# A depthwise convolution shared by four engines: fp32 taps lead on TensorE, VectorE goes on in its bank, and one more low part comes by transfer

## The chip, the cores and the metric

The kernel runs on one core of a Trainium2 chip. The metric is device time in microseconds, from one launch; lower is better. Engines: TensorE (PE, with its weight loads as PEld), VectorE (DVE), ScalarE (ACT), GpSimd (POOL) and SyncE (SP), which issues loads. SBUF and PSUM have 128 partitions; PSUM has 8 banks of 512 fp32 columns.

## The reference

A decoder trunk over 512 positions of 1024 channels, in fp32, two layers, each a token mixer and a gated ConvFFN. Only the first mixer matters here:

```python
def conformer_conv_module(x, w_in, b_in, w_dw, b_dw, ln_g, ln_b, w_out, b_out):
    h = x @ w_in + b_in
    a, gate = jnp.split(h, 2, axis=-1)
    h = a * jax.nn.sigmoid(gate)
    h = causal_depthwise_conv(h, w_dw, b_dw)     # 31 taps over positions, each channel by itself
    h = jax.nn.silu(layer_norm(h, ln_g, ln_b))
    return h @ w_out + b_out
```

After it come the residual norm, the first ConvFFN, the gMLP mixer and the second ConvFFN.

## The kernel before, in words

**Products in split precision.** A matmul of fp32 accuracy is written as three products of `float32r` parts: each operand has a high part (`wh`, `xh`: a copy rounded to float32r) and a low part (`wl`, `xl`: the rest). The weights come in 160-odd units of 128 x 1024. A unit is loaded by SP into one of four slots of `raw` (L464), its high part is made by ScalarE (`his`, L668 to L676), its low part either by a VectorE subtraction (`los`, L1045) or, for the units in `BY_DMA` (L94; 5 to 17), so: ScalarE also writes the negated rounded copy into `wl` (L676), and an accumulating transfer issued by GpSimd (`lo`, L538 to L541) adds `raw` to it. SP loads unit u into its slot only once the low part of unit u - 4 is there (`lo_of`).

**The convolution stage** has eight tiles of 128 channels. Units 2j (gate) and 2j + 1 (value) make tile j: 24 products of 512 columns each, into banks 0 to 2 in turn (`unit_conv`, L1652). ScalarE takes the sigmoid (L773), VectorE multiplies (`gated_channels`, L1080) into `glu[j % 2]`, 30 zeros ahead of 512 positions. The 31 taps of the tile are then shared:

- TensorE has the last `PE_TAPS[j]` taps (5, and 8 in tile 6) as products with diagonal matrices, three products a tap from the split parts `gluh`, `glul`, `diagh`, `diagl` (`taps`, L1683 to L1702), into bank 4 + j % 2.
- VectorE has 17 taps, alternately in banks 6 and 3 (L1108, L1111, L1114), each reading and writing its bank.
- ScalarE makes 9 products (6 in tile 6) into SBUF (`products`, L733), and GpSimd adds them into `gsum` (L550).
- VectorE closes the tile: `gsum` plus its two banks (L1125), plus TensorE's bank, into `cbuf` (L1132; counted by `conv_c`). It also makes `glul` (L1086) from ScalarE's `gluh` (L786).
- TensorE transposes `cbuf` (`to_tm`, L1709) and ScalarE copies that out to `ctm` (L758).

The diagonal matrices of tiles 0 and 1 come from GpSimd (L568), the others from ScalarE, two halves a tap (L713, L714). Tile 7 has its own code, in two halves of 256 positions (`last_taps`, `last_products`, `add_last`, `own_taps`): 17 and 20 taps on TensorE, whose diagonals GpSimd makes for 15 taps (`POOL_LAST`) and ScalarE for the rest. Behind it stand the norm's statistics, the transposes back to feature order (`to_fm`, L1765), silu and its parts (L834, L837, L1205), and the output product (L1618 to L1620).

**What sets the order** is each engine's program as written out by hand, with semaphores between them. TensorE runs unit 2, unit 3, unit 4, `taps(0)`, unit 5 and so on (the loop at the end of the listing). SP's queue in the first 22 us holds the first units, x, parameters, and then the residual's four `res` tiles (L487) and three broadcast rows (L488 to L490).

## Time and profile before

| | us |
|---|---|
| median of 3 runs (lowest, highest) | 1035.72 (1035.41, 1037.11) |
| the profiled execution | 1036.58 |
| its span, first to last instruction | 1034.6 |
| TensorE busy in the span | 1022.5 (99%) |
| VectorE busy | 812.4 (79%) |
| ScalarE busy | 513.0 (50%) |
| GpSimd busy | 233.9 (23%) |
| granted TensorE clock, mean | 0.999 of full speed |
| HBM read, written | 178.11 MB, 54.53 MB |

The span is what the profile covers; the 2 us beside it lie around the first and last instruction. Matmuls are pipelined: a record runs from its start to a modelled end, so that starts, not durations, give their cost. A line number is that of the listing. Times within the span count from its start.

### The profile page before, as it was taken

What the parts mean: (1) busy time and instruction counts of PE and PEld (TensorE: products, weight loads), DVE (VectorE), ACT (ScalarE), POOL (GpSimd) and SP (SyncE); (2) the same over time, 40 slices, a digit from 0 to 9 for tenths busy, and PEclk for the clock granted to TensorE, in tenths of its full rate; (3) what the DMA queues carried; (4) which work ended last, traced back from release to release, by engine and by line L of the source; (5) the groups of instructions that cost most, each with busy time, mean ns of one, the idle gap of its engine ahead of it and who ended that gap; (6) DMA issues with size and microseconds to landing.
All of it is one profiled execution on the core that took longest, in us unless ns stands there. A gap on an engine that the chain in (4) does not pass through costs nothing.

```text
span 1034.6 us, 14305 instructions
## 1 busy us (share of the span) xinstructions
PE 1022.5 (99%) x4799; PEld 854.8 (83%) x4799; DVE 812.4 (79%) x1163; ACT 513.0 (50%) x773; POOL 233.9 (23%) x286
## 2 busy tenths in 40 slices
PE   8999999999999999999999999999999999999997
PEld 7788888988888888888888888898888888888885
DVE  6999977687777776788895778758777677778888
ACT  6899965334343333466553443333433343346553
POOL 2988750413341000000010110042334000000001
PEclk9999999999999999999999999999999999999999
DMA  9566349999998233286555433879999623327653
GB/s 336 169 161 154 91 120 311 227 245 278 229 254 203 84 101 101 82 284 203 186 183 183 140 102 107 305 159 269 282 232 248 168 81 101 101 82 264 203 190 115
DMA packets 65003, 189.70 MB, mean 183 GB/s; under 512 B 7488, under 2 KB 8512, under 8 KB 64960
## 3 DMA queue, kind: packets, MB, share of 16 engines
q1 hardware_dynamic: 44144, 137.76, 39.0%
q0 software_dynamic: 18800, 44.05, 21.8%
q10 hardware_dynamic: 2016, 7.34, 2.1%
q8 instruction: 24, 0.39, 0.2%
q14 instruction: 19, 0.16, 0.0%
HBM read 178.11 MB, written 54.53 MB: 225 GB/s over the span
## 4 chain that ended last, share of the span: by engine, by line
PE 92%; DVE 4%; DMA 1%; issue 1%; ACT 1%; SPq 1%; POOL 0%; DVEq 0%; POOLq 0%; ACTq 0%
PE ps L1608 19%; PE ps L1610 19%; PE ps L1609 19%; PE ps L1851 6%; PE ps L1849 6%; PE ps L1850 6%; PE ps L1618 4%; PE ps L1620 4%; PE ps L1619 4%; DMA raw<-d_weights 1%; PE ps L1779 1%; DVE ps L1114 1%; PE ps L1700 1%; PE ps L1701 1%; PE ps L1699 1%
## 5 line engine op out<-in xcount | busy, mean ns | idle before, releaser
L1608 PE MATMUL ps<-xh,wh 128*128 128x512 f32 x816 | 317.7, 389 | 0.3 <-DVE wl L1045 0.3
L1609 PE MATMUL ps<-xl,wh 128*128 128x512 f32 x816 | 317.5, 389 | 0.0
L1610 PE MATMUL ps<-xh,wl 128*128 128x512 f32 x816 | 317.5, 389 | 0.0
L1608 PEld LDWEIGHTS ps<-xh,wh 128*128 128x128 f32 x816 | 153.2, 188 | 32.3 <-DVE wl L1045 0.8
L1610 PEld LDWEIGHTS ps<-xh,wl 128*128 128x128 f32 x816 | 153.2, 188 | 32.0
L1609 PEld LDWEIGHTS ps<-xl,wh 128*128 128x128 f32 x816 | 153.2, 188 | 31.8
L674 ACT ACTIVATE wh<-raw 128x1024 fp32r<-128x1024 f32 x114 | 119.9, 1056 | 81.7 <-PE ps L1851 63.4
L1045 DVE TENSOR_TENSOR wl<-raw,wh 128x1024 fp32r<-128x1024 f32 x101 | 122.9, 1222 | 41.9 <-ACT wh L674 41.9
L528 POOL TENSOR_SCALAR veps<-sqs 128x1 f32<-128x1 f32 x15 | 5.7, 380 | 554.1 <-ACT squares L849 554.1
L1341 DVE TENSOR_TENSOR wl<-raw,wh 128x1024 fp32r<-128x1024 f32 x80 | 97.6, 1220 | 7.7 <-ACT wh L903 7.6
L1851 PE MATMUL ps<-wh,parts 128*128 128x512 f32 x264 | 102.7, 389 | 0.0
L1849 PE MATMUL ps<-wh,parts 128*128 128x512 f32 x264 | 102.7, 389 | 0.0
L1850 PE MATMUL ps<-wl,parts 128*128 128x512 f32 x264 | 102.7, 389 | 0.0
L886 ACT ACTIVATE vpad<-ps,par 128x512 f32<-128x512 f32 x44 | 30.3, 690 | 143.2 <-PE ps L1610 140.9
L615 POOL DMA_DIRECT2D summed<-d_weights x88 | 73.5, 1100 | 107.8 <-DMA summed<-d_weights 94.5
L894 ACT ACTIVATE parts<-made (+1 forms) x44 | 18.4, 418 | 134.7 <-DVE made L1320 134.7
L903 ACT ACTIVATE wh<-raw 128x1024 fp32r<-128x1024 f32 x80 | 84.1, 1051 | 2.1 <-DMA raw<-d_weights 2.1
L1313 DVE SCALAR_TENSOR_TENSOR gacc<-gpad,par,gacc 128x512 f32<-128x512 f32 x88 | 66.1, 752 | 12.7 <-DVE gacc L1309 6.2
L1313 DVE SCALAR_TENSOR_TENSOR vacc<-vpad,par,vacc 128x512 f32<-128x512 f32 x88 | 66.1, 752 | 11.9
L550 POOL TENSOR_TENSOR gsum<-gsum,prods 128x512 f32<-128x512 f32 x53 | 69.4, 1309 | 10.4 <-ACT prods L733 4.0
L1114 DVE SCALAR_TENSOR_TENSOR ps<-glu,par,ps 128x512 f32<-128x512 f32 x105 | 70.0, 747 | 0.0
L1309 DVE TENSOR_SCALAR vacc<-vpad,par 128x512 f32<-128x512 f32 x44 | 24.0, 546 | 46.6 <-ACT vpad L886 46.6
(201 smaller groups left out, 1738.3 us busy)
## 6 DMA issues: line engine op xcount, KB each, us to landing
raw<-d_weights SPq DMA_DIRECT2D x156, 512.0 KB, 4.1
raw<-summed SPq DMA_DIRECT2D x56, 512.0 KB, 3.4
summed<-d_weights POOLq DMA_DIRECT2D x88, 256.0 KB, 8.6
summed<-d_weights SPq DMA_DIRECT2D x66, 256.0 KB, 7.9
summed<-summed POOLq DMA_DIRECT2D x46, 256.0 KB, 5.1
wl<-raw POOLq DMA_DIRECT2D x13, 512.0 KB, 5.0
...
```

Of the source, the lines that this page charges most:

```text
L674: eng.activation(split_at(u)[0], raw[:, u % RAW, :], ACT.Copy).then_inc(w_hi, 1)
L903: eng.activation(wh[:, slot, :], raw[:, part, :], ACT.Copy).then_inc(w_hi, 1)
L1045: eng.tensor_tensor(l, raw[:, u % RAW, :], h.bitcast(f32), ALU.subtract).then_inc(w_lo, 1)
L1114: eng.scalar_tensor_tensor(out=own[k % 2], in0=glu[:, j % 2, k:k + SEQ], scalar=par[:, c:c + 1], in1=own[k % 2], op0=ALU.mult, op1=ALU.add ...
L1313: eng.scalar_tensor_tensor(out=sums_v[:, :], in0=buf[:, off:off + SEQ], scalar=par[:, bass.ds(cw, 1)], in1=sums_v[:, :], op0=ALU.mult, op1 ...
L1341: eng.tensor_tensor(wl[:, slot, :], raw[:, part, :], wh[:, slot, :].bitcast(f32), ALU.subtract).then_inc(w_lo, 1)
L1608: eng.matmul(ps[:, bank, cols], a, xh[:, k, cols], start=(k == 0), stop=False)
L1609: eng.matmul(ps[:, bank, cols], a, xl[:, k, cols], start=False, stop=False)
L1610: mm = eng.matmul(ps[:, bank, cols], b, xh[:, k, cols], start=False, stop=(k == KD - 1))
L1849: eng.matmul(ps[:, bank + t, :], s_h, w_h[:, cols], start=first, stop=False)
L1850: eng.matmul(ps[:, bank + t, :], s_h, w_l[:, cols], start=False, stop=False)
L1851: mm = eng.matmul(ps[:, bank + t, :], s_l, w_h[:, cols], start=False, stop=last)
```

## The change

Tile 0 has no taps on TensorE, tiles 1 to 5 have three and tile 6 eight, each as one fp32 product (`diagf` with `glu`) ahead of the units, not behind them. VectorE goes on with its taps in TensorE's bank (`CHAIN`) and in one bank of its own (`SUMS[j % 2]`), which ScalarE begins with one tap (`begun`); in tile 0 ScalarE begins both banks. VectorE gates tile j + 1 before the last two taps of tile j, and closes a tile in two steps (`close_sum`, `close_chain`), the second after the first tap of the next tile. `gluh`, `glul`, `diagh` and `diagl` remain for tile 7 alone. The low part of unit 4 too comes by transfer, and units 6 to 15 have one transfer for two units. TensorE now runs units 2, 3, 4 and then, for j from 1 to 5, taps of tile j, unit 2j + 3, `to_tm(j - 1)`, unit 2j + 4; then unit 15, taps of tile 6, `to_tm(5)`. The diff, cut to its core:

```diff
-PE_TAPS = [5, 5, 5, 5, 5, 5, 8] + [20]
+CHAINED = KD - 2
+PE_TAPS = [0] + [3] * (CHAINED - 1) + [8] + [20]
 GP_TAPS = [9, 9, 9, 9, 9, 9, 6]
...
-LAST_AT = 11
-UNIT_4_AT = 10
-
-POOL_TILES = 2
+LAST_AT = 10
...
-BY_DMA = range(LEAD + 2, U_CONV_OUT + 2)
+BY_DMA = range(LEAD + 1, U_CONV_OUT + 2)
+
+LO_DMAS = [[LEAD + 1], [LEAD + 2]] + [[u, u + 1] for u in range(LEAD + 3, U_CONV_OUT, 2)] + [[U_CONV_OUT], [U_CONV_OUT + 1]]
+LO_DMA = {u: d for d in LO_DMAS for u in d}
...
     SUMS = (6, 3)
+    CHAIN = (4, 5)
     CT = 7
...
-            eng.wait_ge(w_neg, u - BY_DMA[0] + 1)
-            eng.dma_start(split_at(u)[1], raw[:, u % RAW, :], accum_op=ALU.add).then_inc(lo_in[u % RAW], 16)
+            n, slot, q = len(LO_DMA[u]), u % RAW, u % RING
+            eng.wait_ge(w_neg, u + n - BY_DMA[0])
+            eng.dma_start(wl[:, q:q + n, :], raw[:, slot:slot + n, :], accum_op=ALU.add).then_inc(lo_in[slot], 16)
 
...
+        n = PE_TAPS[1]
+        w = par[:, C_CDW_W + TAPS + PE_FROM[1]:C_CDW_W + 2 * TAPS].rearrange("p (n o) -> p n o", o=1).broadcast_to([P, n, P])
+        eng.wait_ge(par_in, 16)
+        eng.affine_select(out=diagf[1][:, 0:n, :], in_=w, compare_op=ALU.is_equal, fill=0.0,
+                          base=0, pattern=[[0, n], [-1, P]], channel_multiplier=1).then_inc(diag_p, 1)
+        add_products(0, range(1, 4))
+        lo(LEAD + 1)
+        add_products(0, range(4, 6))
+        lo(LEAD + 2)
+        add_products(0, range(6, GP_TAPS[0]))
         eng.wait_ge(dw_ok, 2)
-        diagonals(0, 0, PE_TAPS[0])
-        add_products(0, range(1, AT_ONCE))
-        diagonals(1, 0, PE_TAPS[1])
-        add_products(0, range(AT_ONCE, GP_TAPS[0]))
-        last_at = PE_TAPS[KD - 3]
+        last_at = 0
         for j in range(1, KD):
-            for u in (2 * j + LEAD, 2 * j + 1 + LEAD):
-                if u in BY_DMA and u < BY_DMA[-1]:
-                    lo(u)
             if j < KD - 1:
+                lo(2 * j + LEAD + 1)
                 add_products(j, range(1, GP_TAPS[j]))
...
+                if j < KD - 1:
+                    if j > 2 and q < PE_TAPS[j - 2]:
+                        eng.wait_ge(dw_pe, j - 2)
+                    last = eng.activation(diagf[j % 2][:, q, :], ident[:, :], ACT.Copy, scale=w)
...
+        def begun(j, k, bank):
+
+            if j == CHAINED:
+                eng.wait_ge(conv_c, j - 1 + k)
+            elif j >= 2:
+                eng.wait_ge(conv_c, j - 1)
+            c = C_CDW_W + j * TAPS + k
+            eng.activation(ps[:, bank, :], glu[:, j % 2, k:k + SEQ], ACT.Copy, scale=par[:, c:c + 1]).then_inc(own_ok, 1)
...
+        sigmoid(0)
+        eng.wait_ge(glu_s, 1)
+        begun(0, 1, SUMS[0])
+        products(0, 0, 2)
+        begun(0, 0, CHAIN[0])
+        products(0, 2, 4)
+        his([LEAD + 1])
+        products(0, 4, 5)
+        his([LEAD + 2])
+        products(0, 5, 7)
+        sigmoid(1)
+        his([LEAD + 3])
+        products(0, 7, GP_TAPS[0])
+        his([LEAD + 4])
+        for j in range(1, CHAINED):
             eng.wait_ge(glu_s, j + 1)
+            begun(j, 0, SUMS[j % 2])
+            products(j, 0, 4)
             if j >= 2:
...
-                his([1 + LEAD])
+            products(j, 4, 6)
...
+            if j + 1 < CHAINED:
+                diagonals(j + 1, range(PE_TAPS[j + 1]))
+            else:
+                diagonals(j + 1, range(PE_TAPS[j + 1] // 2))
+            products(j, 6, GP_TAPS[j] - 1)
+            sigmoid(j + 1)
+            his([2 * j + LEAD + 3])
+            products(j, GP_TAPS[j] - 1, GP_TAPS[j])
+            if j + 1 < CHAINED:
+                his([2 * j + LEAD + 4])
+            else:
+                diagonals(j + 1, range(PE_TAPS[j + 1] // 2, PE_TAPS[j + 1]))
+        j = CHAINED
+        eng.wait_ge(glu_s, j + 1)
+        begun(j, 0, SUMS[0])
+        products(j, 0, 2)
+        begun(j, 1, SUMS[1])
+        products(j, 2, 3)
+        ct_out(j - 2)
+        products(j, 3, AT_ONCE)
+        diagonals(j + 1, range(sum(POOL_LAST), sum(POOL_LAST) + 2))
+        sigmoid(KD - 1)
+        products(j, AT_ONCE, GP_TAPS[j])
+        diagonals(j + 1, range(sum(POOL_LAST) + 2, PE_TAPS[KD - 1]))
         eng.wait_ge(glu_s, KD)
...
+        def chain_of(j):
+
+            if j == 0:
+                return [(k, SUMS[0] if k % 2 else CHAIN[0]) for k in [3] + [k + d for k in range(2, DV_TAPS[0] - 2, 2) for d in (3, 0)] + [DV_TAPS[0] - 2]]
+            if j == CHAINED:
+                return [(k, SUMS[k % 2]) for k in [2, 4, 3] + list(range(5, DV_TAPS[j]))]
+            return [(k, SUMS[j % 2] if k % 2 else CHAIN[j % 2]) for k in range(1, DV_TAPS[j])]
+
...
+        def close_sum(j):
+
+            bank = SUMS[j % 2]
+            eng.wait_ge(dw_tap, ended[j, bank])
             eng.wait_ge(gp_add, adds_before(j + 1))
-            for part in own:
-                n = stat(eng.tensor_tensor(gsum[:, j % 2, :], part, gsum[:, j % 2, :], ALU.add))
-                if part is own[0] and 0 < j < KD - 2:
-                    gated_low(j + 1)
-                eng.wait_ge(st_ok, n)
-            eng.wait_ge(dw_pe, j + 1)
+            return stat(eng.tensor_tensor(gsum[:, j % 2, :], ps[:, bank, :], gsum[:, j % 2, :], ALU.add))
+
+        def close_chain(j, n):
+
+            bank = CHAIN[j % 2]
+            c = C_CDW_B + j
+            eng.wait_ge(dw_tap, ended[j, bank])
+            eng.wait_ge(st_ok, n)
             if j >= 2:
                 eng.wait_ge(ct_pe, j - 1)
-            eng.tensor_tensor(cbuf[:, j % 2, :], gsum[:, j % 2, :], pe_bank, ALU.add).then_inc(conv_c, 1)
+            eng.scalar_tensor_tensor(out=cbuf[:, j % 2, :], in0=gsum[:, j % 2, :], scalar=par[:, c:c + 1],
+                                     in1=ps[:, bank, :], op0=ALU.add, op1=ALU.add).then_inc(conv_c, 1)
+
+        gated_channels(0)
+        los([LEAD])
+        n = None
+        begun_of = {(0, SUMS[0]): 1, (0, CHAIN[0]): 2, (CHAINED, SUMS[0]): CHAINED + 2, (CHAINED, SUMS[1]): CHAINED + 3}
+        for j in range(CHAINED + 1):
+            chain = chain_of(j)
+            for i, (k, bank) in enumerate(chain):
+                c = C_CDW_W + j * TAPS + k
+                if j < CHAINED and i == len(chain) - 2:
+                    gated_channels(j + 1)
+                if j == CHAINED and k == LAST_AT:
+                    gated_channels(KD - 1)
+                if j == CHAINED and k == LAST_AT + 2:
+                    gated_low(KD - 1)
+                if (j, bank) in ended:
+                    eng.wait_ge(dw_tap, ended[j, bank])
+                elif 0 < j < CHAINED and bank == CHAIN[j % 2]:
+                    eng.wait_ge(dw_pe, j)
+                else:
+                    eng.wait_ge(own_ok, begun_of.get((j, bank), j + 2))
+                eng.wait_ge(glu_s, j + 1)
+                eng.scalar_tensor_tensor(out=ps[:, bank, :], in0=glu[:, j % 2, k:k + SEQ], scalar=par[:, c:c + 1],
+                                         in1=ps[:, bank, :], op0=ALU.mult, op1=ALU.add).then_inc(dw_tap, 1)
+                taps_before += 1
+                ended[j, bank] = taps_before
+                if j > 0 and i == 0:
+                    close_chain(j - 1, n)
+            if j < CHAINED:
+                n = close_sum(j)
+
+        j = CHAINED
+        eng.wait_ge(gp_add, adds_before(j + 1))
+        for bank in SUMS:
+            eng.wait_ge(dw_tap, ended[j, bank])
+            n = stat(eng.tensor_tensor(gsum[:, j % 2, :], ps[:, bank, :], gsum[:, j % 2, :], ALU.add))
+            eng.wait_ge(st_ok, n)
+        eng.wait_ge(dw_pe, j)
+        eng.wait_ge(ct_pe, j - 1)
+        c = C_CDW_B + j
+        eng.scalar_tensor_tensor(out=cbuf[:, j % 2, :], in0=gsum[:, j % 2, :], scalar=par[:, c:c + 1],
+                                 in1=ps[:, CHAIN[j % 2], :], op0=ALU.add, op1=ALU.add).then_inc(conv_c, 1)
...
+        def first_taps(j):
+
+            eng.wait_ge(glu_s, j + 1)
+            if j == 1:
+                eng.wait_ge(diag_p, 1)
...
+                eng.wait_ge(diag, j - 1)
                 eng.wait_ge(conv_c, j - 1)
             b, n = j % 2, PE_TAPS[j]
...
                 k = PE_FROM[j] + q
-                eng.matmul(ps[:, 4 + b, :], diagh[b][:, q, :], gluh[:, b, k:k + SEQ], start=(q == 0), stop=False)
-                eng.matmul(ps[:, 4 + b, :], diagh[b][:, q, :], glul[:, b, k:k + SEQ], start=False, stop=False)
-                mm = eng.matmul(ps[:, 4 + b, :], diagl[b][:, q, :], gluh[:, b, k:k + SEQ], start=False, stop=(q == n - 1))
+                mm = eng.matmul(ps[:, CHAIN[b], :], diagf[b][:, q, :], glu[:, b, k:k + SEQ],
+                                start=(q == 0), stop=(q == n - 1))
             mm.then_inc(dw_pe, 1)
...
-        for j in range(1, KD):
-            unit_conv(2 * j)
-            if j in (1, KD - 1):
-                unit_conv(2 * j + 1)
-            if j >= 2:
-                to_tm(j - 2)
-            taps(j - 1)
-            if 1 < j < KD - 1:
-                unit_conv(2 * j + 1)
+        unit_conv(2)
+        unit_conv(3)
+        unit_conv(4)
+        for j in range(1, CHAINED):
+            first_taps(j)
+            unit_conv(2 * j + 3)
+            to_tm(j - 1)
+            unit_conv(2 * j + 4)
+        unit_conv(2 * KD - 1)
+        first_taps(CHAINED)
+        to_tm(CHAINED - 1)
...
```

## Rows read from the trace of the kernel before

**Rows 1.** By stretch: length, busy us of PE, PEld, DVE, ACT, POOL, clock, DMA share, GB/s

```profile
53.32:118.12 64.80, 64.80 (x293) 53.45 (x292) 64.10 (x98) 62.60 (x122) 55.45 (x50) 1.00 0.60 148
```

**Rows 2.** Waits of TensorE, 0 to 150 us: total, times, longest

```profile
PE ps L1618 <- DVE xl L1205: 1.2, 1, 1.2
```

**Rows 3.** Timeline of TensorE: start us, us, engine, line, what

```profile
28.89 0.40 PE L1699 MATMUL ps<-gluh,diagh 128*128 128x512 f32 x1
...
53.32 0.60 PE L1709 MATMUL ps<-ident,cbuf 128*128 128x128 f32 x4
53.67 0.48 PE L1699 MATMUL ps<-gluh,diagh 128*128 128x512 f32 x1
...
57.27 0.39 PE L1608 MATMUL ps<-xh,wh 128*128 128x512 f32 x1
...
68.16 0.60 PE L1709 MATMUL ps<-ident,cbuf 128*128 128x128 f32 x4
...
124.22 0.28 PE L1726 MATMUL ps<-gluh,diagh 128*128 128x256 f32 x1
...
126.73 0.60 PE L1709 MATMUL ps<-ident,cbuf 128*128 128x128 f32 x4
...
136.32 0.38 PE L1765 MATMUL ps<-ident,ctm 128*128 128x128 f32 x2
```

**Rows 4.** Timeline of VectorE

```profile
54.27 9.96 DVE L1114 SCALAR_TENSOR_TENSOR ps<-glu,par,ps 128x512 f32<-128x512 f32 x15
...
124.16 1.42 DVE L1125 TENSOR_TENSOR gsum<-ps,gsum 128x512 f32<-128x512 f32 x2
125.61 0.69 DVE L1132 TENSOR_TENSOR cbuf<-gsum,ps 128x512 f32<-128x512 f32 x1
```

**Rows 5.** Timeline of ScalarE

```profile
18.16 0.67 ACT L773 ACTIVATE sig<-ps,par 128x512 f32<-128x512 f32 x1
...
21.36 2.55 ACT L733 ACTIVATE prods<-glu,par 128x512 f32<-128x512 f32 x4
...
60.72 1.04 ACT L674 ACTIVATE wh<-raw 128x1024 fp32r<-128x1024 f32 x1
61.67 1.04 ACT L676 ACTIVATE wl<-raw 128x1024 fp32r<-128x1024 f32 x1
62.61 0.67 ACT L773 ACTIVATE sig<-ps,par 128x512 f32<-128x512 f32 x1
...
98.39 0.39 ACT L713 ACTIVATE diagh<-ident,par 128x128 fp32r<-128x128 f32 x1
98.68 0.39 ACT L714 ACTIVATE diagl<-ident,dwl 128x128 fp32r<-128x128 f32 x1
```

**Rows 6.** Timeline of GpSimd

```profile
50.20 1.74 POOL L541 DMA_DIRECT2D wl<-raw  x2
52.24 11.38 POOL L550 TENSOR_TENSOR gsum<-gsum,prods 128x512 f32<-128x512 f32 x8 [0.31 <-ACT prods L733]
```

**Rows 7.** The page, part 5: weight loads of the units

```profile
L1608 PEld LDWEIGHTS ps<-xh,wh 128*128 128x128 f32 x816 | 153.2, 188 | 32.3 <-DVE wl L1045 0.8
```

**Rows 8.** Low-part transfers issued from 50 to 52 us, and their landing

```profile
DMA to landing us min/median/max: 4.4/5.5/6.6
```

**Rows 9.** The table by stretch, columns as in rows 1

```profile
20.00:29.50 9.50, 9.50 (x43) 7.85 (x43) 9.46 (x15) 8.29 (x13) 7.03 (x7) 1.00 1.02 411
```

**Rows 10.** The low-part transfer issued at 111.8 us

```profile
DMA to landing us min/median/max: 7.3/7.3/7.3
```

**Rows 11.** The table by stretch at the end of the span

```profile
1031.00:1032.00 1.00, 0.00 (x0) 0.00 (x0) 0.85 (x2) 0.00 (x0) 0.00 (x0) 0.98 0.00 0
1032.00:1033.00 1.00, 0.00 (x0) 0.00 (x0) 0.00 (x0) 0.00 (x0) 0.00 (x0) 0.50 0.95 369
```

**Rows 12.** Timeline of TensorE, start and end of the span

```profile
1.61 3.59 PE L1743 MATMUL ps<-ident 128*128 128x128 f32 x18 [1.61 <-POOL ident L535]
...
1027.16 0.39 PE L1896 MATMUL ps<-xh,parts 128*128 128x512 f32 x1
```

More of the change, by code:

```diff
@@ L412, in lo_of @@
         if u in BY_DMA:
-            return lo_in[u % RAW], 16 * ((u - BY_DMA[0]) // RAW + 1)
+            slot = LO_DMA[u][0] % RAW
+            return lo_in[slot], 16 * sum(d[0] % RAW == slot and d[0] <= u for d in LO_DMAS)
         return w_lo, u + 1 - (len(BY_DMA) if u >= BY_DMA[0] else 0)
@@ L799, in _ @@
                 eng.activation(brow[:, :], brow[:, :], ACT.Copy, scale=1.0 / ALPHA).then_inc(bo1_ok, 1)
-            ahead = []
-            if POOL_TILES <= j + 1 < KD - 1:
-                ahead = list(range(PE_TAPS[j + 1]))
-            elif j + 1 == KD - 1:
-                ahead = list(range(PE_TAPS[KD - 3])) + list(range(PE_TAPS[KD - 3] + sum(POOL_LAST), PE_TAPS[KD - 1]))
-            for i in range(AT_ONCE, GP_TAPS[j]):
-                diagonals(j + 1, ahead[:2])
-                ahead = ahead[2:]
-                if j == KD - 2 and i == GP_TAPS[j] - 1:
-                    sigmoid(KD - 1)
-                products(j, i, i + 1)
-            if ahead:
-                diagonals(j + 1, ahead)
+            if j + 1 < CHAINED:
[22 more added lines that the diff above has]
+        diagonals(j + 1, range(sum(POOL_LAST) + 2, PE_TAPS[KD - 1]))
         eng.wait_ge(glu_s, KD)
-        eng.wait_ge(dw_pe, KD - 2)
         eng.activation(gluh[:, 1, PAD:CW], glu[:, 1, PAD:CW], ACT.Copy).then_inc(glu_hi, 1)
@@ L1714, in last_taps @@
             j = KD - 1
[L1715 to L1717 removed]
+            eng.wait_ge(glu_lo, 1)
+            eng.wait_ge(diag, j - 1)
+            eng.wait_ge(diag_p, 1 + len(POOL_LAST))
             eng.wait_ge(conv_c, j - 1 + h)
```

92 lines of the change are left out of this document (16 added, 76 removed).

## The prediction, made before the changed kernel had been run

> **What bounds the kernel now.** I read the busy times of the page first; they put TensorE far ahead of the others over the whole span. A share of the whole says little about one stage, so the table by stretch comes next: in the stretch of the steady convolution tiles TensorE is full, but VectorE is busy 64.10 and ScalarE 62.60 of the same 64.80 us [rows 1]. Three engines are nearly level there. The waits of TensorE break the tie: in the first 150 us, the start apart, it had one wait to speak of, 1.2 us for `xl`, behind the last tile [rows 2]. So TensorE's own instructions set the pace, with VectorE close behind.
>
> Its timeline gives the price list [rows 3]. A tile is 14.84 us (53.32 to 68.16): 0.35 for four transposes, 3.60 for five taps of three products (0.24 a product), 10.89 for two units (0.227 a product, 5.45 a unit). VectorE's timeline [rows 4]: 15 taps last 9.96 us with the last one's whole 0.75, so 0.658 each from start to start, 9.87 in all; a gate, or the closing of a sum, 0.6 to 0.7. ScalarE [rows 5]: a product 0.61, a high part 0.95 and a negated copy 0.95, a sigmoid 0.57, one half of a diagonal 0.29. GpSimd [rows 6]: eight adds in 11.38.
>
> **The profiled execution** took 1036.58 us (span 1034.6), 0.86 above the median of the runs. My times are on its clock; I subtract the gain from the median.
>
> **TensorE's taps.** 38 taps of tiles 0 to 6, at 0.70 to 0.72 us, go; 23 come (3 each in tiles 1 to 5, 8 in tile 6), each one fp32 matmul of 512 columns. No row shows such a matmul. Below it lie the transposes of fp32 data, 128 columns in 0.0875 us, so 0.35 for 512. Above it I put four full products and two weight loads that nothing hides: 4 x 0.24 + 2 x 0.19 [rows 3, 7] = 1.34. A full-precision product has four partial products where the old code writes out three, so I take four at the unit's spacing: 4 x 0.2275 = 0.91. Three taps are then 2.73 instead of 3.60, and the steady tile is 10.89 + 0.35 + 2.73 = 13.97 us.
>
> The Trainium skill, "FP8 and Floating Point Precision", "TensorE Precision Notes", says that true FP32 makes four passes through the array. No run here shows it, and it leaves my term as it is.
>
> **VectorE and the cycle it now forms with TensorE.** A tile 1 to 5 costs it 18 taps, a gate and two closings: 11.84 + 0.66 + 0.61 + 0.66 = 13.77 us, against 14.6 before; it loses the low part of `glu`. But its second tap waits for PE's taps of the same tile. From there: end of PE's taps + 0.16 (a matmul's record ends 0.39 after its start, spacing 0.23 [rows 3]), 15 taps 9.87, gate 0.74, and PE's next taps can start. That is 2.73 + 10.8 = 13.5 us, under 13.97. TensorE still sets the pace, with 0.4 us to spare.
>
> **ScalarE and GpSimd.** ScalarE's tile falls from some 13.9 to 11.9 us: seven of ten diagonal halves and `gluh` leave, one begun bank comes. GpSimd keeps 11.38 of adds, 1.2 of diagonals for the last tile and 0.9 to 1.75 for one issue of two units in place of two issues; at most 14.3 against 14.0, and its adds of tile 1 end near 47.9, where VectorE wants them at 51.8, so even 0.3 us lost in each of four tiles ends no wait. Its pair of low parts is issued about when TensorE starts the tile; the pair's first unit is needed 2.73 + 5.45 + 0.35 = 8.5 us later. Two separate transfers, issued at 50.20 and 0.6 later, have landed 7.2 us after the first issue [rows 6, 8], so the margin is 1.3 us. SP's loads behind them come 7 us before ScalarE wants them.
>
> **Unit 4, where time is lost.** TensorE ends unit 3 at 28.89 [rows 3] and no longer has taps of tile 0 to do; it asks for unit 4 at once, 3.5 us earlier than now. Its low part was a VectorE subtraction that was ready in time; now it is a transfer. ScalarE's first sigmoid ends at 18.83 [rows 5]; the gate, now ahead of a low part, ends at 19.6; two begun banks and four products (six times 0.61 to 0.63) last to 23.35, high part and negated copy to 25.3. GpSimd adds from 21.6, three times 1.42, and issues at 25.85. SP has queued two `res` tiles and three rows by then, and the 16 DMA engines stand at 102% until 29.5 [rows 9]. A transfer that had them alone took 4.4 us, those that shared them 6.6 and 7.3 [rows 8, 10]. I take 6.6, from the rows of a transfer that had another beside it for part of its way: 32.45. TensorE idles 3.56 us. (The low part of unit 5, issued near 30, isn't needed before 40.6.)
>
> **The sum.** PE's first taps of tile 1 start at 32.45 + 5.45 = 37.9; VectorE has gated tile 1 by 33.2. Four tiles on, taps of tile 5 start at 93.8. VectorE goes on at 96.7, ends gate 6 at 107.3, and closes chain 5 at 110.55. Only then ScalarE may begin the second bank (0.63), and it has a product, a copy of `ctm`, two products, two diagonal pairs, the sigmoid, a product, three pairs and `gluh` to do (0.61 + 0.48 + 1.22 + 1.17 + 0.57 + 0.61 + 1.76 + 0.63 = 7.05): 118.2. VectorE waits some 1 us for it, then low part, five taps, two sums and `cbuf`: 0.6 + 3.3 + 2.2 gives 124.4, where it was 126.30 [rows 4]. TensorE meanwhile: 93.8 + 2.73 + three units + 0.35 = 113.2, eight taps 7.28, transposes 0.35: the last tile starts at 120.8 instead of 124.22, but its first transposes wait for `cbuf`: 124.4 instead of 126.73. From there to the first transpose into feature order it is 9.59 us of TensorE [rows 3], or VectorE's chain, now 1.9 earlier. So 1.9 us are gained at 136, and nothing after it gives them back: TensorE waits once more in the rest of the stage [rows 2], behind the same chain, which moves with it. Forecast: 1035.72 - 1.9 = **1033.8 us**. A measurement of this kernel can tell about 0.2%, or 2.07 us, from no change; the forecast lies just inside.
>
> **Rivals.**
> - *The first transfer is not slowed.* It lands after 4.4 us, at 30.25; TensorE idles 1.4 us. Gain 1.9 + 2.2 = 4.1: 1031.6. For: a transfer with none beside it took that long [rows 8]. Against: the engines are full just then [rows 9]. The Trainium skill, "DMA: Bandwidth & Descriptors", "Anatomy of one DMA", fits 2.0 us + bytes / 436 GB/s, an estimate of 3.2 us for 512 KB, with which the idle time would be near zero and the gain about 5.3; the trace shows 4.4 for the same size [rows 8] and so disagrees. Chance 0.17.
> - *The idle 3.6 us let the clock fall.* In the trace TensorE's last matmul starts at 1027.16, and the granted clock is 1.00 until 1031, 0.98 in the next microsecond, then 0.50 [rows 11, 12], the lower of its two levels (1.2 of 2.4 GHz): it held for some 4 us of idleness, hardly longer than this one. At the start of the kernel 18 transposes took 3.59 us, 0.2 each against 0.0875 later [rows 3, 12], so about 1.8 us were lost. Gain 0.1: 1035.6. The Trainium skill, "TensorE: Matmul & The Clock Gate", "Why this matters for your kernels", warns of idle gaps between bursts for this reason; the trace agrees that the clock falls after one [rows 11]. Chance 0.12.
> - *An fp32 tap is dear* (the rival on the other side). Its place is PE's taps, its price the upper bound, 1.3 us. The path through VectorE holds 15 such taps before gate 6: 15 x 0.4 = 6.0 us more, so 4.1 slower: 1039.8. It decides from 1.04 us a tap. For: weight loads of fp32 are 0.19 us [rows 7] and may not overlap within such an instruction. Chance 0.10.
> - *VectorE becomes the bound.* Each tap now has two semaphores to wait for. If its spacing goes from 0.658 to the 0.72 of sums that wait for each other (124.16 to 125.61 for two) [rows 4], the cycle is 2.73 + 0.95 + 10.8 = 14.5, 0.5 over TensorE's, four times, and tiles 5 and 6 add 1.4: 1.5 slower, 1037.2. Against: the waits can be read while the tap before runs. Chance 0.06.
> - *An fp32 tap is cheap* (0.35 to 0.6). Then TensorE is no bound and VectorE's 13.77 us are, so only 0.2 a tile and some 0.4 at the end come on top: 1032.6. Chance 0.05.
>
> **How the numbers follow.** The forecast's mechanism has the remaining 0.50, with its own range 1032.3 to 1035.5 from a landing of 5.8 to 7.6 us and a tap of 0.86 to 0.96. Faster than 2.07 us: 0.22 of that case, the quick transfer 0.17, the cheap tap 0.05, together 0.44. Slower: the dear tap 0.10, half of VectorE's case and a remainder, 0.14. The rest, 0.42, is the same. For 8 in 10 the range runs from the quick transfer (1031.3) to VectorE's case (1037.3) and leaves out the dear tap.
>
> **What to look for after.** A PE row `ps<-glu,diagf` with spacing near 0.91; tile spacing near 14.0; one wait of TensorE near 29 us of 3.6 us for the transfer into `wl`, and no other before `cbuf` of tile 6 (about 1 us); granted clock 1.00 through it; VectorE waiting for `gluh` once near 117; `cbuf` 6 near 124.4. A wait of TensorE at each tile's second unit would say the paired transfers are late; a VectorE row with idle time for ScalarE's begun banks in every tile would put the bound where I have none.

## The result, and the profile after

The changed kernel takes 1038.41 us (median, 1036.94 to 1040.08); the kernel before, run beside it on the same chip, 1036.64. The ratio is 1.0015, with a 95% interval of 1.0008 to 1.0022: some 1.6 us slower, within the 0.2% that the prediction called "the same". The forecast was 1.9 us faster, and the median lies above its range of 1031.3 to 1037.3. Part of the distance is not the change's: the kernel before now has a median 0.9 us above the 1035.72 that the forecast started from, and 1.0015 times 1035.72 is 1037.3, the range's upper end.

The profiled execution took 1038.23 us, span 1036.5. TensorE's waits in the first 150 us, where before there was one of over 1 us [rows 2] beside that of the start (us in total, times, longest):

```profile
PE ps L1667 <- DMA wl<-raw: 5.7, 1, 5.7
PE ps L1796 <- POOL ident L540: 1.6, 1, 1.6
PE ps L1762 <- DVE cbuf L1190: 1.3, 1, 1.3
PE ps L1677 <- DVE xl L1264: 1.2, 1, 1.2
```

The first line is the news: TensorE stands for 5.7 us until unit 4's low part has landed. The third is the wait for tile 6's `cbuf` that the prediction had at 1. TensorE's timeline, for [rows 3]:

```profile
28.34 0.39 PE L1669 MATMUL ps<-xh,wl 128*128 128x512 f32 x1
34.39 0.79 PE L1667 MATMUL ps<-xh,wh 128*128 128x512 f32 x1 [5.66 <-DMA wl<-raw]
...
41.52 2.74 PE L1753 MATMUL ps<-glu,diagf 128*128 128x512 f32 x6
...
55.51 2.74 PE L1753 MATMUL ps<-glu,diagf 128*128 128x512 f32 x6
...
63.55 0.60 PE L1762 MATMUL ps<-ident,cbuf 128*128 128x128 f32 x4
...
69.48 2.74 PE L1753 MATMUL ps<-glu,diagf 128*128 128x512 f32 x6
...
97.44 2.74 PE L1753 MATMUL ps<-glu,diagf 128*128 128x512 f32 x6
...
128.16 0.66 PE L1762 MATMUL ps<-ident,cbuf 128*128 128x128 f32 x4 [1.29 <-DVE cbuf L1190]
...
137.80 0.38 PE L1820 MATMUL ps<-ident,ctm 128*128 128x128 f32 x2
```

Three taps are six records, two a tap. From them to the transposes, with one unit between, it is 63.55 - 55.51 = 8.04 us; less 5.45 for the unit that is 0.86 a tap. The steady tile is (97.44 - 41.52) / 4 = 13.98 us, 0.86 less than before. So tiles gain what they should, and lose nothing to VectorE. But tile 1 starts 3.6 us late (41.52, forecast 37.9), more than all the gain. Unit 4 started late (34.39, forecast 32.45), and then took 7.13 us (34.39 to 41.52) where a unit needs 5.45. The table by stretch says why it took so long (columns as in [rows 1]):

```profile
30.00:31.00 1.00, 0.00 (x0) 0.00 (x0) 1.00 (x3) 1.00 (x3) 1.00 (x2) 0.93 1.06 246
31.00:32.00 1.00, 0.00 (x0) 0.00 (x0) 1.00 (x3) 1.00 (x3) 0.71 (x2) 0.50 1.03 213
...
36.00:37.00 1.00, 1.00 (x4) 0.81 (x3) 0.51 (x1) 1.00 (x2) 0.93 (x1) 0.50 1.06 332
37.00:38.00 1.00, 1.00 (x4) 0.76 (x4) 0.00 (x0) 1.00 (x3) 0.86 (x2) 0.66 1.13 229
38.00:39.00 1.00, 1.00 (x6) 0.78 (x5) 0.00 (x0) 1.00 (x4) 0.86 (x2) 1.00 1.16 250
```

The granted clock fell to its lower level (0.50, 1.2 GHz) while TensorE stood, and stayed there until 37.7, over the first eight products of unit 4. VectorE's timeline, for [rows 4]:

```profile
44.29 9.98 DVE L1172 SCALAR_TENSOR_TENSOR ps<-glu,par,ps 128x512 f32<-128x512 f32 x15 [7.78 <-PE ps L1753]
...
121.81 0.69 DVE L1119 TENSOR_TENSOR glul<-glu,gluh 128x512 fp32r<-128x512 f32 x1 [0.81 <-ACT gluh L848]
...
127.36 0.75 DVE L1190 SCALAR_TENSOR_TENSOR cbuf<-gsum,par,ps 128x512 f32<-128x512 f32 x1
```

Its taps keep their spacing of 0.658. Last the transfers. GpSimd's timeline has the issue of unit 4's low part at 25.31; then the transfers of 25 to 30 us by queue (packets, MB, share of 16 engines) and the issues of that window (KB, median us to landing). Queue 1 carries SP's transfers, queue 0 GpSimd's:

```profile
25.31 1.09 POOL L547 DMA_DIRECT2D wl<-raw  x1
```

```profile
q1 hardware_dynamic: 461, 1.65, 90.6%
q0 software_dynamic: 33, 0.14, 13.5%
...
wl<-raw POOLq DMA_DIRECT2D x2, 512.0 KB, 8.3
```

The two of that last line are units 4 and 5, 9.0 and 7.5 us. In flight beside them were SP's last `res` tile (landed at 27.0) and its three rows (28.3, 29.4 and 33.4), and GpSimd's queue got 33 packets of the 494 that moved. The mean over the five microseconds hides when. From 25 to 28 us GpSimd's queue moved none at all; the two stretches below are 28 to 29 and 31 to 32 us:

```profile
q1 hardware_dynamic: 86, 0.32, 89.8%
q0 software_dynamic: 2, 0.01, 4.1%
...
q0 software_dynamic: 56, 0.19, 97.6%
q1 hardware_dynamic: 6, 0.02, 5.6%
```

So the transfer was not slowed all along: it waited, 3.6 us from its issue to its first packet, until SP's backlog was nearly through. It landed at 34.3, 0.9 us after the last of SP's rows.

### The profile page after: what moved, and what is told of

It reads as the page before. It is cut to its first block, busy times and chain, and to the rows that moved or that the text cites. A ratio compares the mean times of both kernels' runs of the same rounds, so it can differ in the third digit from the quotient of the medians.

```text
span 1036.5 us, 14240 instructions
## 1 busy us (share of the span) xinstructions
PE 1018.5 (98%) x4731; PEld 844.1 (81%) x4731; DVE 806.6 (78%) x1155; ACT 505.2 (49%) x740; POOL 223.6 (22%) x279
## 4 chain that ended last, share of the span: by engine, by line
PE 83%; DVE 3%; ACT 1%; issue 1%; DMA 1%; POOL 0%; DVEq 0%; POOLq 0%; ACTq 0%
PE ps L1667 17%; PE ps L1668 17%; PE ps L1669 17%; PE ps L1906 6%; PE ps L1904 6%; PE ps L1905 6%; PE ps L1677 4%; PE ps L1679 4%; PE ps L1678 4%; PE ps L1834 1%; DMA raw<-d_weights 1%; PE ps L1949 1%; PE ps L1951 1%; DVE wl L1078 1%; PE ps L1950 1%
## 5 line engine op out<-in xcount | busy, mean ns | idle before, releaser
L1667 PE MATMUL ps<-xh,wh 128*128 128x512 f32 x816 | 321.1, 394 | 5.8 <-DMA wl<-raw 5.7
L1172 DVE SCALAR_TENSOR_TENSOR ps<-glu,par,ps 128x512 f32<-128x512 f32 x125 | 84.7, 750 | 8.5 <-PE ps L1753 7.8
```

What stands on the lines that cost most here:

```text
L1172: eng.scalar_tensor_tensor(out=ps[:, bank, :], in0=glu[:, j % 2, k:k + SEQ], scalar=par[:, c:c + 1], in1=ps[:, bank, :], op0=ALU.mult, op1 ...
L1667: eng.matmul(ps[:, bank, cols], a, xh[:, k, cols], start=(k == 0), stop=False)
```

## The experiments

Two theories stood against each other first. Mine: the low part of unit 4 starves behind SP's backlog, the clock falls for it, and the two undo a gain that is otherwise as forecast. The rival: the tiles' gain is given back behind, where TensorE waits for `cbuf` of tile 6 and VectorE for ScalarE. Ratios are to the kernel before on the same chip; 0.001 is 1.04 us. The start varies by some 2 us from one profiled execution to the next (unit 3 ends between 28.6 and 30.5), so between traces I compare lengths, not times of day. The code cuts below are shortened: `...` and words stand for what is left out.

| experiment | median us | ratio (95% interval) |
|---|---|---|
| the change | 1038.41 | 1.0015 (1.0008, 1.0022) |
| 1 rows later | 1034.85 | 0.9981 (0.9972, 0.9990) |
| 2 unit 4 on VectorE | 1032.84 | 0.9961 (0.9947, 0.9975) |
| 3 TensorE kept busy | 1036.43 | 0.9996 (0.9987, 1.0005) |
| 4 both 1 and 2 | 1032.88 | 0.9956 (0.9942, 0.9969) |
| 5 diagonals ahead | 1039.40 | 1.0026 (1.0017, 1.0035) |
| 6 gate earlier (on 2) | 1032.90 | 0.9967 (0.9955, 0.9979) |
| 7 single transfers (on 2) | 1032.58 | 0.9966 (0.9952, 0.9980) |
| 8 two taps (on 2) | 1036.07 | 0.9998 (0.9989, 1.0007) |
| 9 only the three rows later | 1037.85 | 1.0012 (1.0003, 1.0021) |
| 10 rows later, kernel before | 1036.55 | 1.0000 (0.9991, 1.0009) |
| 11 all together (on 2) | 1031.72 | 0.9955 (0.9941, 0.9968) |
| 12 rows last | 1041.46 | 1.0050 (1.0036, 1.0064) |
| 13 9 with single transfers | 1032.92 | 0.9964 (0.9951, 0.9978) |
| 14 rows last, `brow` in the middle | 1033.34 | 0.9963 (0.9949, 0.9977) |
| 15 14 with the tail of 11 | 1032.41 | 0.9948 (0.9932, 0.9963) |

### 1. SP's other transfers later

```diff
-            t = u - RAW
-            eng.dma_start(res[:, t, :], ...)
-        eng.dma_start(brow ...); eng.dma_start(grow ...); eng.dma_start(brow_n ...)
         for u in range(2 * RAW, UNITS):
             load(u % RAW, u)
+            if 2 * RAW <= u < 3 * RAW: res tile u - 2 * RAW
+            if u == 2 * RAW: brow
+            if u == 3 * RAW: grow, brow_n
```

> The changed kernel, with SP's four loads of res tiles issued behind the loads of units 8 to 11 and the three row broadcasts behind those of units 8 and 12, not ahead of unit 8. Theory (queue): the low part of unit 4 landed 9.0 us after its issue because SP's backlog held the 16 DMA engines until about 31 us. Without it, it lands in 4.4 to 5.5 us (30 to 31 us on the span's clock), TensorE idles 1.3 to 2.5 us instead of 5.7, the granted clock stays at 1.00, and the kernel takes 5 to 6 us less than the changed one (3.5 to 4.5 less than the one before). Rival (own cost): the transfer is slow by itself, while ScalarE, GpSimd and TensorE are all busy; then landing stays near 9 us, TensorE idles above 5 us and the time stays within 1 us of the changed kernel.

Unit 4's low part now landed 4.7 us after its issue, TensorE stood for 1.24 us and its clock did not fall, as the theory had it. The time is 3.5 us below the changed kernel's by the ratios and 2.0 below that of the kernel before: 5 to 6 and 3.5 to 4.5 were expected, so the cause is confirmed and the gain fell short. TensorE's timeline shows where most of the rest is:

```profile
46.55 0.50 PE L1670 MATMUL ps<-xh,wh 128*128 128x512 f32 x1 [1.26 <-DMA wl<-raw]
```

The changed kernel had no such wait: here the pair of units 6 and 7, issued at 35.76, landed 10.7 us later. I come back to it in 9.

### 2 and 4. Unit 4's low part on VectorE again

```diff
-BY_DMA = range(LEAD + 1, U_CONV_OUT + 2)
+BY_DMA = range(LEAD + 2, U_CONV_OUT + 2)
 ...
-        lo(LEAD + 1)
 ...
+                if j == 0 and i == 6:
+                    los([LEAD + 1])
```

> The changed kernel with unit 4's low part again made by VectorE (a subtraction after six taps of tile 0), all else as changed. Theory (queue and clock): TensorE starts unit 4 at once at 28.6; first taps of tile 1 start near 34.2 instead of 41.5. If nothing else binds, 7 us less than the changed kernel. But the low parts of units 5 and of 6 and 7 are then wanted at 36.8 and 42.5, while they landed at 36.7 and 45.5: if those landings don't come earlier by themselves, a wait of up to 3 us appears at unit 6, and the gain is 4 to 5 us. Rival (the stage is bound elsewhere, TensorE's stall only filled time that VectorE or GpSimd needed anyway): less than 2 us gained.

> Unit 4's low part on VectorE and SP's res tiles and rows behind units 8 to 12. Theory: no transfer is late any more (unit 5 lands near 33, units 6 and 7 near 42), TensorE has no wait before cbuf of tile 6, and the kernel takes 7 to 7.5 us less than the changed one, 5.5 less than the one before. Rival (something else in the stage binds once the stall is gone, such as ScalarE's products or GpSimd's adds of tile 1): a new wait on TensorE in tiles 1 or 2, and no more gained than in the better of the two single edits.

2 is 4.0 us below the kernel before and 5.6 below the changed one, 4 is 4.6 and 6.1 below; their intervals overlap, so with unit 4 off the queue nothing shows that SP's order still matters. For 2 this lies between its two cases (4 to 5, or 7); the wait at unit 6 that it feared did not come, since the pair landed after 8.1 us. For 4, 7 to 7.5 us were expected, and its rival is what came: a new wait in tile 1 and no more gained than by 2 alone. One line of the second's timeline shows it: VectorE, with a subtraction more, gates tile 1 late.

```profile
35.63 2.84 PE L1754 MATMUL ps<-glu,diagf 128*128 128x512 f32 x6 [0.86 <-DVE glu L1112]
```

### 3. TensorE kept busy in the gap

```diff
         unit_conv(3)
+        busy(50, CT)
         unit_conv(4)
```

> The changed kernel with 50 transposes of the identity into the free bank 7 between unit 3 and unit 4, some 5.5 us of work that nobody reads. Theory: the transfer still lands at 34.3, but the granted clock stays at 1.00, so the products of unit 4 have a spacing of 0.23 us from the first on instead of 0.43 for the first eight: 1.6 us less than the changed kernel, about the time of the kernel before. Rival (the fall of the clock is harmless, since VectorE or another engine bounds tile 1): no difference above 0.3 us.

Fifty transposes into a bank not in use fill the gap; the landing (9.0 us) stays as it was. Timeline and table by stretch:

```profile
29.13 5.62 PE L1796 MATMUL ps<-ident 128*128 128x128 f32 x50
34.87 0.50 PE L1667 MATMUL ps<-xh,wh 128*128 128x512 f32 x1
```

```profile
28.50:35.00 6.50, 6.39 (x55) 5.98 (x54) 6.44 (x10) 6.50 (x9) 6.00 (x5) 1.00 1.05 262
```

The clock stays at 1.00, and unit 4 takes 5.57 us (34.87 to 40.44) where it took 7.13. That prices the fall at 1.56 us between these two traces; the ratios say 0.0019, 2.0 us (1.6 expected). Delay and clock are thus two costs, and each is about as large as the forecast's gain.

### 5. The rival: the chain behind the tiles

```diff
+                diagonals(KD - 1, range(sum(POOL_LAST), sum(POOL_LAST) + 3))
         j = CHAINED
         ...
         products(j, 0, 2)
+        diagonals(j + 1, range(sum(POOL_LAST) + 3, PE_TAPS[KD - 1]))
         begun(j, 1, SUMS[1])
         ...
-        diagonals(...)  # both later calls
```

> The changed kernel; ScalarE's diagonals of the last tile moved: three taps' worth to the end of its tile 5, where it idles 2.4 us, and two into the wait for closing chain 5 (1.3 us), so that in tile 6 gluh follows the last product at once. Theory (ScalarE's list delays cbuf of tile 6): VectorE's wait of 0.8 us for gluh goes, TensorE's wait for cbuf falls from 1.3 to 0.5 us, 0.8 us less than the changed kernel. Rival (GpSimd's adds of the last tile or the chain behind it bind): less than 0.3 us.

The wait for `cbuf` fell from 1.3 to 0.43 us, and from tile 1's first taps to tile 6's transposes it is 85.79 us instead of 86.64. No gain came of it: 0.8 us less than the changed kernel was expected, and by ratio it is 1.1 us more, with intervals that overlap. ScalarE's timeline, and VectorE's:

```profile
130.99 1.28 ACT L693 ACT_TABLE_LOAD   x1
...
134.29 0.58 ACT L780 ACTIVATE ctm<-ps 128x512 f32<-128x512 f32 x1
```

```profile
134.97 1.02 DVE L1196 BATCH_NORM_STATS2 stats<-ctm 128x6 f32<-128x384 f32 x2 [0.86 <-ACT ctm L780]
```

VectorE waits the 0.86 us for a copy that ScalarE has queued behind its table load and unit 17's rounding. From tile 1's taps to the first `ctm` it is 95.30 us, against 95.40. So behind the tiles two chains are equal, and easing one of them gives nothing; the rival is right about this term, but it is no loss of the change.

This trace shows one thing more, which nothing in the edit asked for. TensorE stood at unit 4 as in the changed kernel, 5.70 us (from 30.3 to 35.99), but the clock did something else (stretches of 34 to 35, 35 to 36 and 41 to 42 us):

```profile
34.00:35.00 1.00, 0.00 (x0) 0.00 (x0) 1.00 (x2) 1.00 (x2) 0.86 (x2) 1.00 1.02 205
35.00:36.00 1.00, 0.01 (x1) 0.02 (x1) 0.96 (x2) 1.00 (x2) 0.98 (x1) 0.54 1.01 201
...
41.00:42.00 1.00, 1.00 (x4) 0.80 (x3) 0.00 (x0) 0.70 (x2) 0.86 (x2) 0.54 1.00 209
```

It held for 4.8 us of the stop where the changed kernel's fell after 2.1, and came back only 5.9 us after TensorE had begun again, so that unit 4 took 8.31 us (35.99 to 44.30) and not 7.13. The same stop cost 2.9 us of clock here and 1.7 there. That is 1.2 us between two single executions that no edit explains, and it is why the price in 3 is better taken from the ratios.

### 6, 7 and 8. What binds once unit 4 is in time

6 puts tile 1's gate four taps before the end of tile 0, 7 issues each unit's low part by itself, 8 takes two taps on TensorE instead of three; all on 2.

```diff
-                if j < CHAINED and i == len(chain) - 2:
+                if j < CHAINED and i == len(chain) - (4 if j == 0 else 2):
```

> The kernel with unit 4 on VectorE, and in tile 0 the gate of tile 1 four taps before the end, not two. There TensorE waited 0.86 us for that gate. Theory: the wait goes and 0.9 us are gained over e2. Rival: TensorE then waits for the low part of unit 5 (landed at 36.3, wanted near 37) or VectorE's closing of tile 0 comes too late, and less than 0.3 us are gained.

The wait at tile 1 is gone, but one of 0.61 us for the gate of tile 2 came in its place. Nothing is gained that these intervals can tell.

```diff
-LO_DMAS = [[LEAD + 2]] + [[u, u + 1] for u in range(LEAD + 3, U_CONV_OUT, 2)] + ...
+LO_DMAS = [[LEAD + 2]] + [[u] for u in range(LEAD + 3, U_CONV_OUT)] + ...
 ...
                 lo(2 * j + LEAD + 1)
+                if 2 * j + LEAD + 2 < U_CONV_OUT:
+                    lo(2 * j + LEAD + 2)
```

> The kernel with unit 4 on VectorE, and one transfer for each of units 5 to 17 instead of pairs. Theory (the pairs' landing is off the path, with 1.2 us to spare in the steady tiles): within 1 us of e2; GpSimd issues 0.9 us more a tile and its adds still end before VectorE wants them. Rival (pairs spare GpSimd what it needs): 2 us or more slower than e2, with VectorE waiting for GpSimd's adds in tiles 3 to 5.

No difference: here the pairs are in time anyway.

```diff
-PE_TAPS = [0] + [3] * (CHAINED - 1) + [8] + [20]
+PE_TAPS = [0] + [2] * (CHAINED - 1) + [8] + [20]
```

> The kernel with unit 4 on VectorE, and two fp32 taps a tile on TensorE in tiles 1 to 5 instead of three; VectorE takes the third. Theory: TensorE's tile would be 13.1 us, VectorE's 13.77 + 0.66 = 14.4; VectorE becomes the bound, tiles are 14.4 us instead of 14.0, and the kernel is 2 us slower than e2. Rival (TensorE alone sets the pace, VectorE has room that the sum does not show): tiles of 13.1 to 13.6 us, 2 to 4 us faster than e2.

```profile
PE ps L1754 <- DVE glu L1112: 5.1, 5, 1.2
PE ps L1763 <- DVE cbuf L1191: 2.8, 1, 2.8
```

A tap less is 0.86 us off TensorE's tile, and the tile grows to 14.56 (49.37 to 63.93): TensorE waits for VectorE's gate in each of them. By ratio it is 3.8 us slower than 2, where 2 us were expected. Four tiles of 0.58 us account for 2.3. The wait for tile 6's `cbuf` is 1.5 us longer than in 2, and behind that stop of 2.83 us the granted clock was at 0.50 from 125.6 to 129.0, which expectation and sum had not. The prediction's second limit is real and near: TensorE sets the pace with three taps, VectorE with two.

### 9 and 10. A smaller dose, and a control

9 leaves the `res` tiles and moves the three rows behind unit 8's load. 10 makes 1's edit in the kernel before, without the change.

```diff
-        eng.dma_start(brow ...); eng.dma_start(grow ...); eng.dma_start(brow_n ...)
         for u in range(2 * RAW, UNITS):
             load(u % RAW, u)
+            if u == 2 * RAW: brow, grow, brow_n
```

> On the changed kernel, SP's three row broadcasts (brow, grow, brow_n) are issued behind unit 8's load; the four residual tiles stay where they are. A smaller dose of the first experiment. Theory (unit 4's low-part transfer starves while SP's own backlog lasts): SP's backlog ends about 27 to 28 us, lo(4) lands 5 to 6.5 us after its issue instead of 9.0, TensorE idles 1.5 to 3 us at unit 4 instead of 5.7, its clock stays at 1.00, and the time is 2 to 4 us below the changed kernel's. Rival (the transfer through GpSimd's queue takes 9 us by itself here, and the first experiment gained for another reason): landing 8 us or more, time within 0.7 us of the changed kernel's.

> Control on the kernel before: only SP's order is changed as in the first experiment (residual tiles with units 8 to 11, row broadcasts later), none of the change. If the reordering gains only by giving way to unit 4's low-part transfer, which this kernel does not have, the time is that of before: ratio 0.999 to 1.001. If the reordering is a gain by itself (raw tiles that arrive earlier), the ratio is 0.998 or less, and the first experiment's gain says nothing of the transfer.

The control is plain: without the change SP's order is worth nothing (1.0000, within 0.9 us either way). The ninth was a miss. Unit 4 landed in 4.7 us, tile 1's taps started at 35.75, 5.8 us earlier than in the changed kernel, and yet the time fell by 0.3 us by ratio, which the intervals can't tell from nothing; 2 to 4 were expected. TensorE's timeline, and the table by stretch:

```profile
47.24 0.80 PE L1668 MATMUL ps<-xh,wh 128*128 128x512 f32 x1 [2.83 <-DMA wl<-raw]
...
54.40 2.74 PE L1754 MATMUL ps<-glu,diagf 128*128 128x512 f32 x6
```

```profile
48.00:49.00 1.00, 1.00 (x4) 0.81 (x3) 1.00 (x2) 1.00 (x2) 0.69 (x2) 0.50 0.70 229
```

The same failure, one transfer further on. The pair of units 6 and 7, issued at 34.89, landed 12.3 us later; TensorE stood 2.83 us, its clock fell just before it began again, and the unit took 7.16 us. The queues from 36 to 41 us, and the landing:

```profile
q1 hardware_dynamic: 349, 1.30, 89.3%
q0 software_dynamic: 16, 0.13, 12.6%
```

```profile
wl<-raw POOLq DMA_DIRECT2D x1, 1024.0 KB, 12.3
```

SP's rows, issued from 30.5 on, had been moved onto the next of GpSimd's transfers. In the changed kernel that pair took 10.8 us too (issued 34.69, landed 45.5), but TensorE was so late that it did not want unit 6 before 49.9: the first delay hid the second.

### 12 to 15. Both transfers free

Open was whether SP's traffic or the size of 1 MB made the pair late. 12 moves the `res` tiles to units 12 to 15, `brow` to unit 12, `grow` and `brow_n` to unit 16.

```diff
-            if 2 * RAW <= u < 3 * RAW: res tile u - 2 * RAW
-            if u == 2 * RAW: brow
-            if u == 3 * RAW: grow, brow_n
+            if 3 * RAW <= u < 4 * RAW: res tile u - 3 * RAW
+            if u == 3 * RAW: brow
+            if u == 4 * RAW: grow, brow_n
```

> The changed kernel with SP's four residual tiles behind the loads of units 12 to 15, brow behind that of unit 12, grow and brow_n behind that of unit 16, so that neither unit 4's low part nor the pair of units 6 and 7 has SP's extra traffic beside it. Theory (SP's traffic starves both transfers): lo(4) lands in 4.5 to 5.5 us, the pair in 7 to 8.5 us, TensorE waits about 1.2 us at unit 4 and not at unit 6, and the time is 1 to 1.6 us below the first experiment's, 3.5 to 5 us below the changed kernel's. Rival (the pair is late by its size, or because the units' own loads run beside it): the pair lands in 10 us or more, TensorE waits over 1 us at unit 6, and the time is the first experiment's within 0.5 us.

The landings were 4.7 and 8.3 us and TensorE did not stand at unit 6, as the theory had it. But the edit made a wait of its own: 3.6 us slower than the changed kernel, not 3.5 to 5 faster, so that its time answers nothing. ScalarE's timeline, then TensorE's:

```profile
66.46 1.06 ACT L825 ACTIVATE brow<-brow 128x1024 f32<-128x1024 f32 x1 [10.77 <-DMA brow<-d_rows]
```

```profile
71.03 5.16 PE L1756 MATMUL ps<-glu,diagf 128*128 128x512 f32 x6 [5.56 <-DVE glu L1116]
```

ScalarE scales `brow` in tile 2, and stood 10.77 us for it with tile 3's sigmoid queued behind.

13 is the ninth with the pairs issued unit by unit (as in 7), and leaves SP's traffic where it was.

> The ninth experiment (three row broadcasts behind unit 8's load) with the pairs of low parts issued one unit at a time, 512 KB each. Theory (starved by SP's traffic whatever its size): unit 6's transfer, issued near 34.9 us, lands later than 8 us after its issue, TensorE still waits 0 to 1.5 us for it at 44.4 us, and the time is 1 to 3 us below the ninth's. Rival (the size of 1 MB made it late): unit 6 lands in 4.5 to 6.5 us, TensorE does not wait at unit 6, and the time is 3 to 4 us below the ninth's.

Unit 6, 512 KB now and issued at 35.39, still landed only when TensorE asked for it:

```profile
45.40 0.50 PE L1670 MATMUL ps<-xh,wh 128*128 128x512 f32 x1 [0.17 <-DMA wl<-raw]
```

That is 10 us for 512 KB, which took 4.7 undisturbed, so half the size alone does not cure the slow landing, and the theory has its landing and its wait. But it came in time, where the pair had not, and no clock was lost: by ratio 5.0 us below the ninth, more than either theory gave. The traces account for 4.4 of them: 2.7 of the stop (2.83 against 0.17) and 1.7 of the clock (7.16 against 5.45). Single transfers thus bring the ninth level with 14 below.

14 is the twelfth with `brow` behind unit 10's load.

```diff
-            if u == 3 * RAW:
+            if u == 2 * RAW + 2:
                 eng.dma_start(brow ...)
```

> As the twelfth experiment, with brow issued behind unit 10's load (near 45 us) so that it lands before ScalarE scales it in tile 2. Theory (SP's traffic starved both transfers and nothing else stood in the way): TensorE waits about 1.2 us at unit 4, under 0.3 us at unit 6 and not for the gate of tile 3, and the time is 1 to 1.6 us below the first experiment's, 3.5 to 5 us below the changed kernel's. Rival (the stop at unit 6 was not on the path, the chains of VectorE or ScalarE set the tiles anyway): time within 0.5 us of the first experiment's.

TensorE's timeline, the queues from 36 to 41 us, and the landing of the pair:

```profile
29.85 0.50 PE L1670 MATMUL ps<-xh,wh 128*128 128x512 f32 x1 [1.27 <-DMA wl<-raw]
...
35.42 2.74 PE L1756 MATMUL ps<-glu,diagf 128*128 128x512 f32 x6
...
49.42 2.74 PE L1756 MATMUL ps<-glu,diagf 128*128 128x512 f32 x6
```

```profile
q0 software_dynamic: 111, 0.91, 93.6%
q1 hardware_dynamic: 80, 0.33, 17.3%
```

```profile
wl<-raw POOLq DMA_DIRECT2D x1, 1024.0 KB, 8.3
```

In the same five microseconds GpSimd's queue moved 0.91 MB instead of the ninth's 0.13, and tile 1 took 14.0 us. By ratio this is 5.4 us below the changed kernel (0.9963 against 1.0015) and 1.9 below 1, both just over the ranges expected, and 3.8 below the one before. Two of its eight executions have a mean clock of 0.996, where the other six have 0.998 or 0.999, and took 1034.98 and 1037.34 us; no trace of these two shows why. It is the change as it stands, every low part of units 4 to 17 by transfer, with nothing but SP's four `res` tiles and three rows given another place.

15 adds the fifth's edit and one line more: ScalarE's copy of tile 6 ahead of the table load. 11 had tried the same on 2, with 6's gate.

```diff
         last_products(1, 0, 4)
+        ct_out(KD - 2)
         table_of(ACT.Silu)
         his([U_CONV_OUT + 1])
-        ct_out(KD - 2)
```

> The fourteenth with ScalarE's five diagonal pairs of tile 7 moved ahead as in the fifth, and its copy of tile 6's transposed output ahead of the table change and of unit 17's rounding. Theory (the copy gave back the fifth's 0.85 us): 0.7 to 1.3 us below the fourteenth. Rival (another chain binds there): within 0.4 us of it.

> The second experiment (unit 4's low part on VectorE) with the gate of tile 1 four taps before the end of tile 0, ScalarE's five diagonal pairs of tile 7 moved ahead as in the fifth, and ScalarE's copy of tile 6's transposed output put ahead of its table change and of unit 17's rounding. Theory (the 0.85 us of the fifth experiment was given back only because that copy stood behind the table change): the wait for cbuf of tile 6 stays under 0.5 us, VectorE's last part no longer waits for ScalarE's copy, and the time is 0.7 to 1.5 us below the sixth experiment's. Rival (something else behind, TensorE's output product or the last statistics, binds at the same time): no gain, within 0.4 us of it.

VectorE's timeline of 15 has its first `ctm` at

```profile
131.15 1.76 DVE L1227 TENSOR_SCALAR ctm<-ctm,mv,rstd 128x128 f32<-128x128 f32 x6 [0.51 <-POOL rstd L525]
```

94.65 us behind tile 1's taps (36.50), where 14 has 95.43 (35.42 to 130.85): 0.8 us gained, the term that the fifth could not cash. By ratio 15 is 1.6 us below 14 and 11 is 1.2 below 6; in both the intervals overlap, so that the runs agree with 0.8 but do not prove it. 15 has the lowest ratio of the study; those of 2, 4 and 11 lie inside its interval.

## Why the prediction was wrong

**The step that failed** is "I take 6.6, from the rows of a transfer that had another beside it for part of its way". It measured 9.0. The rows taken [rows 8] had one neighbour for part of their way; here the neighbour was SP's backlog, and the row that showed it stood in the prediction [rows 9]. The price supposed that the transfer would go on, only slower, beside it. It did not. In 9, with the rows away, its first packets moved at 27.0 us, 1.5 after the issue; here at 28.9, 3.6 after it, and over 25 to 30 us GpSimd's queue had 13.5% of the engines' time against 90.6%. With the issue 0.5 us earlier than forecast, unit 4 began 1.94 us late. Experiments 1, 9, 12, 13 and 14 show the cause: with SP's rows out of its way the same transfer takes 4.7 in each, in 9 and 13 although the `res` tiles stayed. The prediction's page rule, 2.0 us + bytes / 436 GB/s from "Anatomy of one DMA" in the Trainium skill's "DMA: Bandwidth & Descriptors", gives an estimate of 3.2 us and is short in both cases. The section "SWDGE vs HWDGE vs iDMA" of the same page of the Trainium skill says that an engine goes round between the internal queues that software and hardware descriptors feed; a first packet 2.1 us later than in 9, and shares of 13.5% and 90.6% over 5 us, do not look like turns of equal weight, and no run here shows how the engines choose.

**The clock was a rival with a chance of 0.12, and came true.** The forecast counted on a clock of 1.00 through the wait. The rival's price was forecast as 1.8 us (its own figures, 18 transposes at 0.2 less 0.0875, give 2.0); it was 1.68 in the changed kernel's trace (7.13 less 5.45), 2.86 in the fifth's and 2.0 by the ratios of experiment 3. I gave it too little because I took the 4 us of idleness at the end of the span [rows 11] for what the clock bears. It bears no fixed time. Counted from TensorE's stop it fell after 2.1 us in the changed kernel, 2.8 in 9, 3.4 in 8 and 12, but 4.8 in 5, and at the end of the changed kernel's span after 4.9. A stop of 3.56 us, my own forecast, lies in the midst of these: in four of these five stops within the work the clock would have fallen, in one not. So a chance of 0.12 was far too small, and forecast and rival should have stood near each other, 1033.8 and 1035.6; which of them comes is, as far as these traces go, chance.

**Together** 1.94 + 1.68 = 3.62 us: tile 1 at 41.52 instead of 37.9. Unit 3 ended 0.32 us earlier than in the trace before (28.57 against 28.89), so counted from there it is 3.94. A gain of 1.9 less 3.9 is a loss of 2.0; from the end of unit 3 to the first transposes into feature order it is 109.23 us instead of 107.43 (137.80 and 136.32 [rows 3]), 1.8 more, and the ratio says 1.6.

**What held.**
- fp32 taps: 0.91 forecast, 0.86 measured, by three taps above and by the eight of tile 6 (116.88 to 123.75); the dear tap, the rival on the slower side, is excluded. 0.86 us is four times 0.215, close to four of the unit's products, though the trace shows two records a tap, not four. The Trainium skill, "FP8 and Floating Point Precision", "TensorE Precision Notes", says four passes; the trace's sum agrees.
- The steady tile: 13.97 forecast, 13.98 measured, and no wait in it. That it fits to 0.01 is luck: the taps are 0.15 us cheaper than forecast, and the unit behind the transposes takes 5.57 (49.94 to 55.51) and not 5.45. VectorE's nearness, 0.4 us, is borne out by 8: one tap more for it, and it sets the pace (14.56). As a rival (sums that wait for each other) it did not come: the spacing stayed 0.658.
- The pairs: margin 1.3 us forecast where they run undisturbed; in 14 the pair, issued at 34.55, has landed at 42.9 and is wanted at 43.8 (35.42 + 8.04 + 0.35), a margin of 0.9. What I missed is that in tile 1 SP's traffic can be there too (9), which the changed kernel's own delay hid.
- The tail: VectorE's wait for `gluh` 0.81 (forecast 1), TensorE's for `cbuf` 1.3 (about 1), `cbuf` 6 closed at 128.1, 3.7 behind the forecast of 124.4, that is by the delay of tile 1 and hardly anything else.
- The quick transfer, 4.4 us and 1031.6, a gain of 4.1: this is what 14 makes of the change, 4.7 us, a stop of 1.27 and a gain of 3.8.
